# Three edits to a decoder trunk kernel: mask and maximum of a strip in one VectorE operation, the narrow column block of the projection first, the sample tile in halves

## The chip, the cores and the metric

The kernel runs on one core of one Trainium2 chip. The metric is the device time in microseconds; the median of the runs is compared. A core has TensorE (PE, matrix products into PSUM), VectorE (DVE), ScalarE (ACT) and GpSimd (POOL), a sync engine (SP) that issues most DMAs, a memory of 128 partitions (SBUF) and eight banks of 512 fp32 columns per partition into which products go (PSUM). All data is fp32.

## The reference, cut to what matters

One layer of a hybrid decoder trunk, for 1024 prompt tokens and 64 sample tokens (8 sequences of 8). Two pieces of it bear on the change. The first is the norm and the one combined input projection, of which the first 1304 columns (queries, keys and values of three branches, gates) are the attention part:

```python
n = rms_norm(x, lp['norm1_g'])
z = n @ lp['w_in']
z_attn, z_gate, z_rwkv = _split(z, [D_ATTN + 6 * D_KV, N_BRANCH * N_HEADS_ATTN, SHIFT_COLS])
```

The second is the sliding-window ("local") branch of prompt attention: a block of 128 queries against the 512 keys before it and its own 128, masked at both ends:

```python
s_w = jnp.einsum('bqghd,bkgd->bghqk', qg, win_kv[:, :, 0].astype(f32))
dist = q_pos[:, None] - w_pos[None, :]
p_w = masked_softmax(s_w, (dist >= 0) & (dist < WINDOW) & (w_pos[None, :] >= 0))
o_w = jnp.einsum('bghqk,bkgd->bqghd', p_w, win_kv[:, :, 1].astype(f32))
```

The rest (RWKV-7 time mixing of eight heads, compressed and selected branches, sample attention over a paged cache, output projection, an MLP of 4096) is computed by parts of the kernel that the change leaves alone.

## The kernel before, in words

Every engine has a program of its own, written out by hand in one order, with semaphores between them. The stages follow each other on TensorE: input projection, attention columns (to about 183 us), projection of the RWKV columns (to about 400), RWKV recurrence, compression of cache pages, prompt attention (850 to 1150), sample attention, output projection, MLP (from 1400 on).

**Projection.** Tokens lie in TILES = 9 tiles: eight of 128 prompt tokens and tile PT = 8 with the 64 sample tokens. The attention columns are in three BLOCKS (L503): 0 to 511, 512 to 1023 and 1024 to 1303. Weights of block b go to buffer b % 2. SP (L570 to L603) issues x tile 0, the norm's gain g1, the weights of block 0, the other x tiles, the weights of block 1, small constants, two weight tiles of the next stage, then waits for the first block's products before it issues the weights of block 2. ScalarE norms a tile (norm_rows, L900: square with sum, Ln, Exp, scaled copy), TensorE transposes it (turn_x, L1301: eight 128x128 transposes into banks 0 and 1, where each half waits until VectorE has read that bank's former tile), VectorE multiplies by g1 and writes nt (L2023). att_group (L1320) then makes the product of one tile and one block: eight k-steps, nt as the stationary operand, into one of three banks in turn; ScalarE evicts it (att_out, L917), which reorders the query columns of block 0. In the pass over the first block, TensorE's order (L1369 to L1374) is: turn tile 0, turn tile 1, group 0, turn tile 2, group 1 and so on. The other two blocks follow without transposes. For a sample tile the product has 64 rows, so half of the array's output columns. VectorE's head_sums(t) (L2042) waits until the third block of tile t is evicted.

**Prompt attention.** For each of eight query tiles i there are two units: "s" (selected branch, all i + 1 key tiles) and "cw" (compressed, then window, at most 5 key tiles). A unit has score steps, one for each pair of heads (two strips, g = 0 and 1, of up to 1024 columns), and the value steps of the unit before are spread between them (the list `order`, L458). With more than four key tiles the two strips fill banks 0 to 3, so the next scores (L1686) wait until both exponentials of the step are done. One step: TensorE writes the scores (L1703); VectorE adds the mask to both strips' edges in one operation (L2337 for full window strips, tiles 4 to 7; L2340 for the others) and takes the negated maximum of each strip (L2343); ScalarE computes exp(score - max) with its sum (exp_strip, L1170, the instruction on L1182). ScalarE's own order puts the two copies of a value step's transposed weights (v_copy, L1161, instruction on L1168) ahead of the first exponential, and where two value steps lie between two score steps the second's copies ahead of the second exponential.

`mm` (L1298) is the helper that issues every product, so products of all stages show as L1299. An fp32 product shows as two MATMUL instructions.

Of the kernel before, what the change touches and what calls it, by code (L numbers as in the profile page):

```python
# [15 lines left out]
P = 128  # L16
# [29 lines left out]
def rows(t):  # L46
    return P if t < PT else NS


def decode_trunk(nc, x_prompt, x_sample, cache_cmp_kv, cache_slc_kv, cache_win_kv, state_wkv, state_shift,  # L50
# [5 lines left out]
    with ctx:  # L56
# [214 lines left out]
        assert at[0] <= W0  # L271
        at[0] = W1
        ptb = [work(512) for _ in range(4)]
        qt = [work(HG, P) for _ in range(2)]
# [227 lines left out]

        BLOCKS = [(0, 512), (512, 512), (1024, ZA - 1024)]  # L503
        SPANS = [(0, 512), (512, 512), (1024, NS)]
# [42 lines left out]
        def _(sp):  # L547
# [21 lines left out]

            load_x(0)  # L570
            with nc.allow_non_contiguous_dma("small vectors, channel on the partition"):
                sp.dma_start(g1, norm1_g[0].rearrange("(k p) -> p k", p=P)).then_inc(sem("g1_in"), 16)
            load_w(0)
            for t in range(1, TILES):
                load_x(t)
# [316 lines left out]
        def _(act):  # L892
# [24 lines left out]
            def att_out(i):  # L917
                b, m = ATT[i]
                act.wait_ge(sem("proj"), i + 1)
                c0, n = BLOCKS[b]  # L920
                out, src = za[0:rows(m), m, c0:c0 + n], banks[2 + i % 3][0:rows(m), 0:n]
                if b == 0:

                    out = out.rearrange("p (h g d) -> p g h d", g=KVH, d=HD)
                    src = src.rearrange("p (g h d) -> p g h d", g=KVH, d=HD)
                nc.scalar.activation(out, src, ACT.Copy).then_inc(sem("att_out"), 1)  # L926
# [243 lines left out]
            def exp_strip(u, s, g):  # L1170
                i, kind = UNITS_A[u]
                x = no_s[u, s]
                act.wait_ge(sem("pa_max"), exps[x] + g + 1)
                if s == "c":
                    nc.scalar.activation(pc_r[i % 2], pc_r[i % 2], ACT.Exp).then_inc(sem("pa_p"), 1)
                    return
                br, hh = s
                if u >= 2 and hh == 0 and g == 0:
                    act.wait_ge(sem("turn_in"), after_unit(u - 2))
                h, w = head_of(hh, g), P * len(key_tiles(i, br))  # L1180
                s0 = strip_at(x)[0][g]
                nc.scalar.activation((pb_w if br else pb_s)[:, h, 0:w], psum[:, s0:s0 + w], ACT.Exp, bias=pmax[:, br, h:h + 1],  # L1182
                                     accum_out=psum_[:, br, h:h + 1]).then_inc(sem("pa_p"), 1)

# [112 lines left out]
        def _(pe):  # L1297
# [22 lines left out]
            def att_group(i):  # L1320
# [5 lines left out]
                ring_free(i)  # L1326
                n = BLOCKS[b][1]
                for k in range(KT):
                    ins = mm(banks[2 + i % 3][0:rows(m), 0:n], nt[:, k, m * P:m * P + rows(m)],
                             wb[b % 2][:, k, 0:n], k == 0, k == KT - 1)  # L1330
# [39 lines left out]
            turn_x(0)  # L1370
            for t in range(TILES):
                if t + 1 < TILES:
                    turn_x(t + 1)
                att_group(t)  # L1374
# [623 lines left out]
        def _(dve):  # L1998
# [313 lines left out]
            nc.vector.engine_nop().then_inc(once("q_zero")[0], 1)  # L2312

            def strip_max(u, s):
                i, kind = UNITS_A[u]
# [19 lines left out]
                if br == 1 and i >= WINDOW // P:  # L2335
                    ends = shaped3(strips, step // WINDOW, WINDOW)[:, :, :, 0:P]
                    link(tt(ends, ends, spread(edge_causal, 1, 2), ALU.add))  # L2337
                else:
                    ends = strips[:, :, w - P:w]
                    link(tt(ends, ends, spread(causal_add, 1, 2), ALU.add))  # L2340
# [278 lines left out]
```

## Time and profile before

| | us |
|---|---|
| median of the runs | 2261.91 (2259.36 to 2263.99, 3 runs) |
| the profiled execution | 2249.74 |
| its span | 2248.0 |
| TensorE busy | 2115.9 (94%) |
| VectorE busy | 1128.7 (50%) |
| ScalarE busy | 628.5 (28%) |
| GpSimd busy | 150.7 (7%) |

Times inside the profile are counted from the span's start. Busy time of TensorE is modelled at the ends of its instructions. An entry such as "x8" gives the number of instructions; "idle before" is the time that the engine stood still ahead of them, with the releaser behind the arrow.

### The profile page before, as it was taken

To read this page: it belongs to the slowest core of one execution; us is meant where nothing else is said; L and a number is where in the kernel's file an instruction comes from. 1 tells how busy PE (TensorE), PEld (TensorE's weight loads), DVE (VectorE), ACT (ScalarE), POOL (GpSimd) and SP (SyncE) were. 2 spreads that over 40 slices of the span, in tenths; PEclk is the share of its full clock that TensorE was granted. 3 is DMA by queue.
4 is the path that set the end of the run, shared out by engine and by line. 5 is a ranking of instruction groups with operands and counts; after the bars stand their busy time and mean duration, and the time that the engine had idled before them with its cause. 6 is when DMAs were issued, how large, how long until landed. Compare 5 with 4: busy or idle time off the path is not lost.

```text
span 2248.0 us, 36929 instructions
## 1 busy us (share of the span) xinstructions
PE 2115.9 (94%) x15228; PEld 1199.6 (53%) x15228; DVE 1128.7 (50%) x2278; ACT 628.5 (28%) x1408; POOL 150.7 (7%) x248
## 2 busy tenths in 40 slices
PE   7999999899998887888887899999999999999999
PEld 4456566799996774444344444444444444444443
DVE  2026664367665446766545313463636354554635
ACT  4113553222322115666543311202020111111110
POOL 3000000122222001211110000000000000000000
PEclk9999999999998997999998999999999999999999
DMA  6000112100012531000035421011111111111101
GB/s 189 21 1 19 29 29 88 68 4 22 4 23 77 170 96 54 10 5 5 5 113 154 129 75 61 11 60 42 38 38 38 38 38 38 38 38 38 38 38 80
DMA packets 99957, 115.72 MB, mean 51 GB/s; under 512 B 32243, under 2 KB 72116, under 8 KB 99726
## 3 DMA queue, kind: packets, MB, share of 16 engines
q1 hardware_dynamic: 95310, 106.01, 15.0%
q10 hardware_dynamic: 4480, 7.34, 1.1%
q8 instruction: 121, 1.98, 0.4%
q14 instruction: 46, 0.38, 0.1%
HBM read 104.75 MB, written 12.64 MB: 52 GB/s over the span
## 4 chain that ended last, share of the span: by engine, by line
PE 83%; DVE 6%; ACT 5%; DMA 2%; issue 2%; SPq 2%; ACTq 1%; POOL 0%; POOLq 0%; DVEq 0%
PE psum L1299 77%; PE psum L1724 2%; ACT arena L1182 2%; ACT arena L1168 1%; DMA arena<-in_cache_cmp_kv_dram 1%; SPq L702 1%; DVE arena L2343 1%; PE psum L1781 1%; PE psum L1622 1%; DVE arena L2369 1%; ACTq L1135 1%; DVE arena L2196 1%; DMA arena<-in_x_prompt_dram 0%; PE psum L1540 0%; SPq L646 0%
## 5 line engine op out<-in xcount | busy, mean ns | idle before, releaser
L1299 PE MATMUL psum<-arena 64*64 64x64 f32 (+12 forms) x12272 | 1863.6, 349 | 76.8 <-ACT arena L1182 44.0
L1299 PEld LDWEIGHTS psum<-arena 64*64 64x64 f32 (+5 forms) x12272 | 969.9, 152 | 872.5 <-issue 677.6
L2523 DVE TENSOR_TENSOR arena<-arena,psum 128x512 f32<-128x512 f32 x48 | 33.0, 688 | 305.8 <-PE psum L1299 305.8
L1280 ACT ACTIVATE arena<-psum 128x512 f32<-128x512 f32 x48 | 28.5, 594 | 420.0 <-PE psum L1299 327.3
L1271 ACT ACTIVATE arena<-arena 128x512 f32<-128x512 f32 x64 | 40.2, 628 | 274.2 <-DVE arena L2533 168.0
L1168 ACT ACTIVATE arena<-psum 128x512 f32<-128x512 f32 (+1 forms) x148 | 80.8, 595 | 86.3 <-PE psum L1724 74.4
L856 POOL TENSOR_TENSOR arena<-arena,m_lev 128x256 f32<-128x256 f32 x82 | 65.3, 797 | 586.2 <-DVE arena L2177 388.8
L1182 ACT ACTIVATE arena<-psum,arena 128x640 f32<-128x640 f32 (+7 forms) x128 | 88.8, 700 | 11.4 <-DVE arena L2343 10.9
L2343 DVE TENSOR_REDUCE arena<-psum 128x1 f32<-128x640 f32 (+7 forms) x128 | 84.6, 703 | 2.2
L2196 DVE TENSOR_TENSOR arena<-arena,psum 128x512 f32<-128x512 f32 x65 | 44.6, 687 | 74.2 <-PE psum L1299 73.5
L1048 ACT ACTIVATE arena<-psum 128x256 f32<-128x256 f32 x82 | 31.5, 384 | 171.4 <-PE psum L1299 171.4
L1724 PEld LDWEIGHTS psum<-ident,arena 128*128 128x128 f32 x528 | 59.1, 145 | 35.0 <-ACT arena L1168 15.4
L1724 PE MATMUL psum<-ident,arena 128*128 128x128 f32 x528 | 75.6, 288 | 2.1 <-DVE arena L2369 1.1
L2506 DVE TENSOR_TENSOR arena<-psum,arena 128x1024 f32<-128x1024 f32 x8 | 9.8, 1225 | 97.8 <-PE psum L1299 97.8
L1622 PE MATMUL psum<-ident,arena 128*128 128x128 f32 x272 | 42.6, 283 | 13.1 <-DVE arena L2266 13.1
L926 ACT ACTIVATE arena<-psum 128x512 f32<-128x512 f32 (+3 forms) x27 | 14.4, 532 | 133.2 <-PE psum L1299 133.2
L886 POOL TENSOR_SCALAR arena<-arena 128x640 f32<-128x640 f32 (+4 forms) x64 | 46.7, 741 | 49.1 <-DVE arena L2366 48.9
L1299 PE MATMUL psum<-ident,arena 64*64 64x64 f32 (+1 forms) x920 | 47.5, 223 | 2.5 <-DVE arena L2177 0.8
L1781 PE MATMUL psum<-ident,arena 128*128 128x128 f32 (+1 forms) x248 | 41.8, 307 | 8.4 <-DMA arena<-in_cache_slc_kv_dram 4.2
L2266 DVE COPY arena<-arena 128x512 f32<-128x512 f32 x68 | 27.9, 457 | 40.8 <-DMA arena<-in_cache_cmp_kv_dram 40.3
L1781 PEld LDWEIGHTS psum<-ident,arena 128*128 128x128 f32 (+1 forms) x248 | 29.5, 152 | 30.6 <-ACT arena L1217 14.6
L1299 PEld LDWEIGHTS psum<-ident,arena 64*64 64x64 f32 (+1 forms) x920 | 42.7, 139 | 4.4 <-DVE arena L2303 1.0
(311 smaller groups left out, 1717.8 us busy)
## 6 DMA issues: line engine op xcount, KB each, us to landing
arena<-in_cache_slc_kv_dram SPq DMA_DIRECT2D x128, 128.0 KB, 2.3
arena<-in_w_up_dram SPq DMA_DIRECT2D x7, 2048.0 KB, 7.4
arena<-in_w_down_dram SPq DMA_DIRECT2D x7, 2048.0 KB, 7.8
arena<-in_cache_cmp_kv_dram SPq DMA_DIRECT2D x72, 128.0 KB, 3.3
arena<-in_x_prompt_dram SPq DMA_DIRECT2D x16, 512.0 KB, 9.5
arena<-in_cache_cmp_kv_dram ACTq DMA_DIRECT2D x56, 128.0 KB, 3.1
arena<-in_w_in_dram SPq DMA_DIRECT2D x13, 512.0 KB, 3.9
arena<-in_w_in_dram SPq DMA_DIRECT2D x2, 2048.0 KB, 14.1
```

Source lines behind the costliest of these rows:

```text
L856: nc.gpsimd.tensor_tensor(amt[:, n % 2], atrb_r[c % 3][:, :, 0, :], spread(m_lev[:, i, :], 1, HP), ALU.mult).then_inc(sem("rw_amt"), 1)
L886: ins = nc.gpsimd.tensor_scalar(pb_w[:, h, 0:w], pb_w[:, h, 0:w], psum_[:, 1, h:h + 1], gates[:, i, 3 * h + 2:3 * h + 3], ALU.mult, ALU.mult)
L1168: nc.scalar.activation(ptb[2 * (st % 2) + g][0:p0], banks[4 + (f + g) % 2][0:p0], ACT.Copy).then_inc(sem("turn_out"), 1)
L1182: nc.scalar.activation((pb_w if br else pb_s)[:, h, 0:w], psum[:, s0:s0 + w], ACT.Exp, bias=pmax[:, br, h:h + 1], accum_out=psum_[:, br, h ...
L1271: link(nc.scalar.activation(block, block, ACT.Relu))
L1299: return nc.tensor.matmul(out, lhsT, rhs, start=start, stop=stop)
L1622: ins = nc.tensor.transpose(banks[g % 4][:, cols], by_head[a][x][:, cols], ident)
L1724: ins = nc.tensor.transpose(b[:, hh * P:(hh + 1) * P], (pb_w if s[0] else pb_s)[:, h, c0:c0 + P], ident)
L1781: ins = nc.tensor.transpose(b[0:t.shape[1], x * P:(x + 1) * P], t, ident)
L2196: tt(flat, flat, banks[4], ALU.subtract).then_inc(sem("rw_t"), 1)
L2343: nc.vector.tensor_reduce(pmax[:, br, h:h + 1], psum[:, s0[g]:s0[g] + w], AX.X, ALU.max, negate=True).then_inc(sem("pa_max"), 1)
L2523: tt(u2, t_sb, bank_of(6), ALU.add).then_inc(sem("u_sum"), 1)
```

## The change

Projection: the narrow block (280 columns) is the first of the three, and the two wide ones follow; x tile 1 is issued ahead of g1 and the weights; TensorE multiplies tile 0 ahead of transposing tile 1; the sample tile's product is made in two halves of the block's columns, one into partitions 0 to 63 and one into 64 to 127 of a bank, alternating k by k, and evicted with two copies. Window strips of tiles 4 to 7: a mask row of 640 columns is built once; one VectorE operation per strip adds it, negates, writes the strip back and gives the minimum, which is the negated maximum; the exponential of those strips takes scale -1.

```diff
+        window_add = region(R0 + HEADS * SEQ + HEADS * (WINDOW + P), WINDOW + P)
...
-        BLOCKS = [(0, 512), (512, 512), (1024, ZA - 1024)]
+        BLOCKS = [(1024, ZA - 1024), (0, 512), (512, 512)]
...
             load_x(0)
+            load_x(1)
...
-            for t in range(1, TILES):
+            for t in range(2, TILES):
                 load_x(t)
...
+                if m == PT:
+                    for h, half in enumerate(HALVES):
+                        out, src = za[0:NS, m, c0 + h * n // 2:c0 + (h + 1) * n // 2], banks[2 + i % 3][half, 0:n // 2]
+                        if c0 == 0:
+                            out = za[0:NS, m, 0:n].rearrange("p (h g d) -> p g h d", g=KVH, d=HD)[:, h]
+                            src = src.rearrange("p (h d) -> p h d", d=HD)
+                        ins = nc.scalar.activation(out, src, ACT.Copy)
+                    ins.then_inc(sem("att_out"), 1)
+                    return
...
+                turned_sign = br == 1 and i >= WINDOW // P
                 nc.scalar.activation((pb_w if br else pb_s)[:, h, 0:w], psum[:, s0:s0 + w], ACT.Exp, bias=pmax[:, br, h:h + 1],
-                                     accum_out=psum_[:, br, h:h + 1]).then_inc(sem("pa_p"), 1)
+                                     scale=-1.0 if turned_sign else 1.0, accum_out=psum_[:, br, h:h + 1]).then_inc(sem("pa_p"), 1)
...
+                if m == PT:
+                    for k in range(KT):
+                        for h, half in enumerate(HALVES):
+                            ins = mm(banks[2 + i % 3][half, 0:n // 2], nt[:, k, SEQ:], wb[b % 2][:, k, h * n // 2:(h + 1) * n // 2],
+                                     k == 0, k == KT - 1)
+                    ins.then_inc(sem("proj"), 1)
+                    return
...
             turn_x(0)
-            for t in range(TILES):
+            att_group(0)
+            turn_x(1)
+            for t in range(1, TILES):
                 if t + 1 < TILES:
                     turn_x(t + 1)
                 att_group(t)
...
+            link(nc.vector.memset(window_add, 0.0))
+            link(nc.vector.tensor_copy(shaped(window_add, WINDOW // P + 1, P)[:, 0::WINDOW // P, :], edge_causal))
...
                 if br == 1 and i >= WINDOW // P:
-                    ends = shaped3(strips, step // WINDOW, WINDOW)[:, :, :, 0:P]
-                    link(tt(ends, ends, spread(edge_causal, 1, 2), ALU.add))
+                    for g in range(KVH):
+                        h, strip = head_of(hh, g), psum[:, s0[g]:s0[g] + w]
+                        nc.vector.tensor_tensor_reduce(strip, strip, window_add, -1.0, -NEG, ALU.add, ALU.min,
+                                                       pmax[:, br, h:h + 1]).then_inc(sem("pa_max"), 1)
+                    return
```

## Rows read from the trace of the kernel before

**Rows 1.** The page: shares of the chain that ended last, by engine.
```profile
PE 83%; DVE 6%; ACT 5%; DMA 2%; issue 2%; SPq 2%; ACTq 1%; POOL 0%; POOLq 0%; DVEq 0%
```

**Rows 2.** Busy time by stretch: start:end, length, engines, granted clock, DMA share, GB/s.
```profile
200.00:300.00 100.00, 98.91 (x444) 59.20 (x443) 71.99 (x188) 55.41 (x142) 0.00 (x0) 1.00 0.12 31
300.00:400.00 100.00, 100.00 (x456) 61.24 (x455) 44.99 (x105) 38.36 (x106) 0.00 (x0) 1.00 0.24 75
...
1000.00:1100.00 100.00, 82.06 (x472) 40.74 (x471) 61.29 (x114) 60.51 (x123) 15.88 (x18) 0.98 0.02 6
```

**Rows 3.** TensorE groups by form, 0 to 175 and all; then timeline pieces.
```profile
L1299 PE MATMUL psum<-arena 128*64 128x512 f32 x32 | 14.2, 595 | 0.0
...
L1299 PE MATMUL psum<-arena 128*128 128x280 f32 x128 | 30.5, 400 | 0.0
...
L1299 PE MATMUL psum<-arena 128*64 128x280 f32 x16 | 4.0, 402 | 0.0
...
1396.79 7.09 PE L1299 MATMUL psum<-arena 128*64 128x512 f32 x32
...
845.99 0.42 PEld L1299 LDWEIGHTS psum<-arena,ident 128*64 128x64 f32 x8 [0.33 <-issue]
846.00 0.66 PE L1299 MATMUL psum<-arena,ident 128*64 128x127 f32 x8
```

**Rows 4.** Chain of waits of the first 160 us: start, length, what.
```profile
2.35 10.03 DMA arena<-in_x_prompt_dram
...
15.34 1.97 PE psum L1309 x8
17.31 7.34 PE psum L1299 x16
24.65 0.87 PE psum L1309 x8
25.52 6.87 PE psum L1299 x16
```

**Rows 5.** Timeline of the start, VectorE: start, length, engine, line.
```profile
8.97 1.44 DVE L2023 TENSOR_TENSOR arena<-psum,g 128x512 f32<-128x512 f32 x2 [3.27 <-PE psum L1309]
```

**Rows 6.** Stretches of 4 us with GB/s last; then issue to landing of the narrow block.
```profile
0.00:4.00 4.00, 0.00 (x0) 0.00 (x0) 1.71 (x7) 1.28 (x1) 2.58 (x17) 1.00 0.49 127
4.00:8.00 4.00, 0.26 (x2) 0.29 (x3) 1.53 (x6) 2.79 (x5) 2.97 (x18) 1.00 1.01 326
8.00:12.00 4.00, 1.68 (x8) 1.28 (x6) 1.38 (x2) 0.00 (x0) 3.32 (x11) 1.00 1.05 409
...
arena<-in_w_in_dram SPq DMA_DIRECT2D x1, 1120.0 KB, 5.1
```

**Rows 7.** VectorE and ScalarE groups by form, 800 to 1160: busy, mean ns, idle before.
```profile
L2343 DVE TENSOR_REDUCE arena<-psum 128x1 f32<-128x640 f32 x40 | 31.1, 820 | 0.7
...
L2337 DVE TENSOR_TENSOR psum<-psum,edge_causal 128x512 f32<-128x512 f32 x16 | 11.2, 700 | 31.7 <-PE psum L1299 31.7
...
L1182 ACT ACTIVATE arena<-psum,arena 128x640 f32<-128x640 f32 x40 | 31.5, 792 | 0.0
```

**Rows 8.** Timeline of one window step of tile 5.
```profile
1017.85 0.70 DVE L2337 TENSOR_TENSOR psum<-psum,edge_causal 128x512 f32<-128x512 f32 x1 [0.79 <-PE psum L1299]
1018.43 1.09 ACT L1168 ACTIVATE arena<-psum 128x512 f32<-128x512 f32 x2 [2.03 <-PE psum L1724]
1018.59 1.56 DVE L2343 TENSOR_REDUCE arena<-psum 128x1 f32<-128x640 f32 x2
...
1019.45 0.79 ACT L1182 ACTIVATE arena<-psum,arena 128x640 f32<-128x640 f32 x1
...
1020.23 0.78 ACT L1182 ACTIVATE arena<-psum,arena 128x640 f32<-128x640 f32 x1
...
1021.16 1.35 PE L1299 MATMUL psum<-arena 64*128 64x512 f32 x8 [1.32 <-ACT arena L1182]
```

**Rows 9.** Timeline around the gate into prompt attention.
```profile
852.64 0.43 DVE L2340 TENSOR_TENSOR psum<-psum,edge_causal 128x256 f32<-128x256 f32 x1 [3.53 <-PE psum L1299]
```

More of the change, by code:

```diff
@@ L272, in decode_trunk @@
         at[0] = W1
+        window_add = region(R0 + HEADS * SEQ + HEADS * (WINDOW + P), WINDOW + P)
+        assert R0 + HEADS * SEQ + (HEADS + 1) * (WINDOW + P) <= W0
         ptb = [work(512) for _ in range(4)]
@@ L920, in att_out @@
                 c0, n = BLOCKS[b]
+                if m == PT:
[7 more added lines that the diff above has]
+                    return
                 out, src = za[0:rows(m), m, c0:c0 + n], banks[2 + i % 3][0:rows(m), 0:n]
-                if b == 0:
+                if c0 == 0:
                     out = out.rearrange("p (h g d) -> p g h d", g=KVH, d=HD)
```

## The prediction

> **What bounds the kernel now.** The head of the page comes first: TensorE is busy 94% of a 2248.0 us span (the table above) and its instructions make up 83% of the chain that ended last; VectorE, which one edit touches, is busy 50% and holds 6% of that chain [rows 1]. The change lives in two places, so the table of stretches is read next, for those places only [rows 2]. In the projections TensorE has no room: 98.91 of 100 us in 200 to 300 and 100.00 in 300 to 400, with VectorE at 71.99 and 44.99. Work taken off TensorE here is therefore time gained, and so is an earlier start. In prompt attention (1000 to 1100) TensorE has 82.06 us of work, VectorE 61.29 and ScalarE 60.51: nobody is full, so a loop of latencies decides, and only the timeline of one step of that loop can tell what a faster VectorE is worth.
>
> The profiled execution took 2249.74 us (2248.0 of span and 1.7 around it), 0.5% under the median of the runs, 2261.91 (2259.36 to 2263.99). I work out differences in the profiled execution and take them off the median. A difference of 0.2% (4.5 us) is about the least that a measurement of this kernel can tell from none.
>
> **Part 1: the sample tile in halves.** Per column block, the sample tile is 8 k-steps whose weights are 128x64; each fp32 product shows as two matmul instructions, so 16 of them. In the first pass 32 such instructions of 512 columns cost 14.2 us, 0.444 each [rows 3], while the 16 of a full 128x128 product take 6.87, 0.43 each [rows 4]: half of the array's columns do nothing. In the narrow block 16 instructions of 280 columns cost 4.0 us. After the change there are 32 instructions per block at half the columns, and halves of the array alternate k by k. The row for that form is the sample tile of the output projection, which already does it: 32 instructions of 512 columns in 7.09 us, 0.222 each [rows 3]. At 256 columns that is 0.111 each, 32 x 0.111 = 3.55 us per wide block against about 6.95 (the average of 6.87 and 7.1); at 140 columns 32 x 0.061 = 1.95 against 4.0. Gain 3.4 + 3.4 + 2.05 = 8.8 us.
> What could spoil it is the doubled number of weight loads. Eight 128x64 loads took 0.42 us, 0.053 each, beside eight products in 0.66 us, 0.083 each [rows 3]. The wide blocks have 0.111 for each load, far enough; the narrow one has 0.061. Bounds: if 0.083 is the floor for the narrow block it takes 2.65 us and the gain is 8.1; if the halves did not overlap at all, each instruction of 256 columns costs half of 0.444 and the gain is zero. I take 8.8, by the row of the same alternation.
> The Trainium skill, "TensorEngine Tiling (Array Packing)", sections Key Properties and Restrictions, speaks against this edit: a change of tiling mode drains TensorE, and column tiling switches the fast weight load off. The sample tile before is 128x64 as well, so by that rule nothing is added but the loads, and the rows put these at 0.053 us; the sum stays as it is.
> Eviction: two ScalarE copies of half the columns instead of one, and ScalarE waits for TensorE there. Nothing.
>
> **Part 2: narrow block first, second x tile ahead of the weights, first product before the second transposes.** Rows 4 and 5 carry this. Before, the chain is: x tile 1 queues behind 2 MB of weights and lands at 12.37, its norm takes until 15.3, transposes 1.97, first product at 17.31 [rows 4]. Tile 0 had been normed and transposed by then and was written by VectorE at 8.97 + 1.44 = 10.41 [rows 5]; then TensorE waited 5 us for tile 1.
> After: tile 1 (0.52 MB) is second in the queue, the weights third and only 1.15 MB. By 4 us the queue had moved 127 x 4 = 0.51 MB, by 8 us another 326 x 4 = 1.30 MB, then 409 GB/s [rows 6]. Tile 1 is complete at 1.05 MB, about 5.7 us; the weights at 2.2 MB, 8 + 0.39/0.409 = 9.0 us. The same block alone took 5.1 us from issue to landing in the trace [rows 6], so short rows are no great handicap; bounds 8.8 to 10.5 (the 5.1 counted from 5.4, when tile 1 is nearly in). The small vector g1 now follows tile 1, about 6.5 us, and is wanted at 8.97. So the first group starts when VectorE has written tile 0, at 10.5.
> It is narrow: 16 x 0.238 = 3.8 us when TensorE is at speed [rows 3]. It won't be: transposes that take 0.87 in the stream took 1.97 at 15.34, and the first group 7.34 against 6.87 [rows 4], 1.57 us lost; the granted clock of this stretch reads 1.00 all the same, so I go by durations. I charge 1.2 us (bounds 0.5 to 1.9): the group ends at 15.5. ScalarE has normed tile 1 from 7.6 to 10.5 and tile 2 by 14. Transposes of tile 1 until 16.4; those of tile 2 share two banks with them, so their halves wait for VectorE's two writes of 0.69 us (16.0 to 17.4): they end at 17.9, with 0.7 us of stall. At 17.9 three tiles are turned and one narrow group is done. Before, at 17.31, two tiles were turned and no group done, and 0.47 us of cold were still to come. Gain: 0.87 + 3.8 + 0.47 - 0.59 = 4.6 us. Bounds 3 (weights at 10.5 and the cold charge at its top) to 5.5.
> Does the faster first pass starve? Its period falls from 6.87 + 0.87 = 7.74 to 3.8 + 0.87 = 4.67 us. ScalarE needs 0.40 to evict and 2.9 to norm a tile, 3.3; VectorE 1.3. x tiles arrive each 1.3 us. Slack 1.4 us. The second block's weights (2.1 MB) stand right behind the x tiles: 7.7 MB in all, 8 + 5.9/0.409 = 22.4 us by the rate of rows 6 (28 if it sags), and they are wanted at about 52. The third block, now 2 MB, is issued when the first pass is done (52) and wanted after the second (111); on SP's queue behind its wait stand only weight loads that wait for later products. The head sums of VectorE need all three blocks of a tile; the last block is now a wide one, so their tiles come every 6.87 us instead of every 3.8 and crowd it less than before (71.99 us busy in 200 to 300, with TensorE nearly full) [rows 2]. Nothing is next in line: the projection ends at about 169.5 instead of 183, and the rest moves up.
>
> **Part 3: mask and maximum in one VectorE operation.** 16 steps (tiles 4 to 7, four each). Removed per step: a mask add over 512 elements, 0.700 us, and two reductions over 640, 0.78 each (0.820 as the table's mean, which counts overlap) [rows 7]; 2.3 us. Added: two operations that read a PSUM strip and an SBUF row, write 640 elements to PSUM and give a minimum. The trace has none. From below: an add of 512 is 0.700 and a reduction of 640 is 0.820 [rows 7]; in pure proportion an add of 640 is 0.875, with a fixed part less, say 0.83; an accumulator read, if it comes as an instruction of its own as on ScalarE, overlaps or adds up to 0.2. From above: a second cycle per element gives 1.5. I take 0.95, nearest to the add.
> What is it worth? One step of the loop [rows 8]: the scores end at 17.8 (1017.8), VectorE adds until 18.55, its first maximum is ready at 19.4, its second at 20.15. ScalarE meanwhile copies two transposed banks, 18.43 to 19.52, starts the first exponential at 19.45, the second at 20.23, and TensorE's next scores wait for that one, 21.16. So the first maximum is hidden by the copies and the second by the first exponential. The table agrees: ScalarE idled 0.0 us before its 40 exponentials of 640 [rows 7]. A step that saves VectorE 0.4 us moves nothing. Value: 0, from -0.1 to +0.1 us per step. The cover is gone when two of the new operations last longer than 20.23 - 17.85 = 2.38 us, 1.19 each; in the 6 steps that have two value steps between their exponentials (1, 2 and 3 in tiles 5, 6 and 7) only past 1.75 each.
> The negated exponential costs the same. The two new operations before the first strip (a memset of 640, a copy of 256; under 1.3 us by the rows of adds) lie in the 3.53 us for which VectorE stood idle before 852.64, its first work in this stage [rows 9]; the gate that TensorE waits for is signalled ahead of them, and between it and 852.64 TensorE transposes, ScalarE copies and TensorE makes scores, some 1.9 us. Nothing.
>
> **Sum.** -8.8 - 4.6 - 0 = -13.4 us: 2261.9 - 13.4 = **2248.5 us**, 0.59% faster (the profiled execution would be 2236.3).
>
> **Rivals.** (a) *Two cycles per element for the fused operation*: 1.5 + 0.1 = 1.6 each, 3.2 per step against 2.38. Ten steps lose 0.8, six lose nothing: +8.2, so 2256.7. For it: it is a two-input operation with an accumulator and the trace shows no such thing; against: one input is in PSUM, and the two-input add of the trace, which reads PSUM and SBUF and writes PSUM too, takes 0.700 us for 512 elements [rows 7]. The Trainium skill, "Vector Engine (DVE) Microarchitecture Reference", section Points that are easy to get wrong, says that an accumulating two-source operation halves its rate when both sources are non-bf16 and in SBUF; here only one is, so by its letter the rule spares this operation, by its reason perhaps not. Chance 0.15.
> (b) *Slower than before: the fused operation takes over the loop.* At T us each the loss is 10(2T - 2.38) + 6(2T - 3.5) = 32T - 44.8; it eats 13.4 us at T = 1.82. At three cycles per element (2.15 us) it is +24, so 2272.5. Nothing in the trace points there; only that its price is unseen. Chance 0.06.
> (c) *The maximum does gate the loop*: then each of 16 steps gains the 0.6 us by which the first maximum is earlier, -9.6, so 2239. The 0.05 us between 19.40 and 19.45 is for it, the 0.0 idle against. Chance 0.06.
> (d) *The halves do not overlap*: -4.6 only, 2257. The row of 7.09 us is against it. Chance 0.05.
>
> **Chances and range.** Forecast 0.68, its own range 2244 to 2254 (the bounds of parts 1 and 2, 1.6 us of part 3 and 2 us of run-to-run median). For 8 in 10 it reaches down toward (c) and up over (a) and (d): 2242 to 2258. Faster by over 0.2% (below 2257.4): forecast, (c), three quarters of (a), half of (d), 0.87; within 0.2%: 0.07; slower: 0.06.
>
> **What would show it.** The products start at 10.5 and not 17.3; the sample group takes 3.5 us in wide blocks; projection ends near 169.5; TensorE stays at 100% to 400 us. In attention, scores still start every 4.71 us in the one-value steps, and ScalarE idles 0.0 before its 640-wide exponentials; VectorE's own busy time falls. If the period grows, the new operation is over 1.19 us; if it shrinks, I read the ScalarE cover wrongly. If weights land after 10.5 or TensorE stays slow longer, part 2 is smaller.

## The result and the profile after

The changed kernel took 2241.78 us (median of 7 runs, 2234.79 to 2247.9) beside 2259.61 for the kernel before (7 runs, 2255.53 to 2265.8): ratio 0.9922, 95% interval 0.9901 to 0.9943, so the medians lie 17.8 us or 0.8% apart. The forecast was 2248.5 with a range of 2242 to 2258: the direction was right, the range was missed by 0.2 us at its low end. More runs, told below, put the effect at 15 us and not 17.8.

The profiled execution took 2245.14 us, with a span of 2243.3. Where before and after can be compared mark by mark, its first 400 us are these:

| | before | predicted | after |
|---|---|---|---|
| first product starts | 17.31 | 10.5 | 10.45 |
| first group of the narrow block ends | | 15.5 | 16.01 |
| second group may start (three tiles turned) | | 17.9 | 18.49 |
| projection of the attention columns evicted | 183.2 | 169.5 | 171.0 |
| end of the projections | 406.6 | | 394.0 |

The chain of the page, the answer to [rows 1], says little: TensorE keeps its 83%, VectorE gives up a point.

```profile
PE 83%; DVE 5%; ACT 5%; issue 2%; DMA 2%; SPq 2%; ACTq 1%; POOL 0%; POOLq 0%; DVEq 0%
```

The chain of waits at the start answers [rows 4] (start, length, what):

```profile
0.82 3.70 DMA arena<-in_x_prompt_dram
...
7.64 1.95 PE psum L1322 x8
9.59 0.02 issue
9.62 0.70 DVE arena L2045
10.32 0.14 issue
10.45 5.56 PE psum L1312 x16
16.01 0.45 PE psum L1322 x4
16.46 0.02 issue
16.49 0.70 DVE arena L2045
17.19 0.14 issue
17.33 1.16 PE psum L1322 x8
18.49 3.78 PE psum L1312 x16
22.26 0.87 PE psum L1322 x8
```

The DMA of x tile 1 has left the chain. What follows tile 0 is VectorE's write of it, then the first group, which takes 5.56 us where the same group in the stream takes 3.78: 1.8 us lost to a TensorE that is not yet at speed, called the cold start below. TensorE's groups by form, 0 to 175 us, answer [rows 3]:

```profile
L1312 PE MATMUL psum<-arena 128*64 128x256 f32 x64 | 7.3, 382 | 0.0
...
L1312 PE MATMUL psum<-arena 128*64 128x140 f32 x32 | 2.1, 286 | 0.0
```

Two wide blocks of the sample tile take 7.3 us together, 3.65 each, and the narrow one 2.1; before, 14.2 and 4.0. The stretches answer [rows 2]; the second one stops being full only because the projections now end at 394:

```profile
200.00:300.00 100.00, 98.90 (x451) 58.52 (x450) 64.92 (x168) 52.68 (x135) 0.00 (x0) 1.00 0.12 32
300.00:400.00 100.00, 96.93 (x494) 60.27 (x494) 44.58 (x107) 34.90 (x102) 0.00 (x0) 1.00 0.27 91
1000.00:1100.00 100.00, 81.95 (x453) 40.06 (x452) 54.98 (x118) 59.73 (x120) 15.95 (x18) 0.97 0.02 6
```

In attention, VectorE fell from 61.29 to 54.98 us in 100, TensorE stands as it was. The groups by form of 800 to 1160 answer [rows 7] (busy, mean ns, idle before):

```profile
L1195 ACT ACTIVATE arena<-psum,arena 128x640 f32<-128x640 f32 x40 | 31.6, 800 | 0.0
...
L2363 DVE CUSTOM_DVE_ANT_0 psum<-psum,arena 128x640 f32<-128x640 f32 x32 | 25.8, 849 | 39.3 <-PE psum L1312 39.3
```

and the timeline of a step in tile 5 answers [rows 8]:

```profile
1003.01 0.83 DVE L2363 CUSTOM_DVE_ANT_0 psum<-psum,arena 128x640 f32<-128x640 f32 x1 [1.13 <-PE psum L1312]
1003.59 1.09 ACT L1180 ACTIVATE arena<-psum 128x512 f32<-128x512 f32 x2 [0.75 <-PE psum L1746]
1003.76 0.14 DVE L2363 DVE_READ_ACCUMULATOR2_ANT arena<- 128x1 f32 x1
1003.76 0.87 DVE L2363 CUSTOM_DVE_ANT_0 psum<-psum,arena 128x640 f32<-128x640 f32 x1
1004.54 0.14 DVE L2363 DVE_READ_ACCUMULATOR2_ANT arena<- 128x1 f32 x1
...
1004.56 0.80 ACT L1195 ACTIVATE arena<-psum,arena 128x640 f32<-128x640 f32 x1
...
1005.33 0.81 ACT L1195 ACTIVATE arena<-psum,arena 128x640 f32<-128x640 f32 x1
...
1006.28 1.35 PE L1312 MATMUL psum<-arena 64*128 64x512 f32 x8 [1.28 <-ACT arena L1195]
```

The first maximum is there at 1003.9, but ScalarE is busy with its copies until 1004.68 (1003.59 + 1.09, of which the last 0.12 overlap with what follows), so the first exponential starts at 1004.56, and TensorE waits for the second. Score steps with one value step between them start every 4.66 us instead of every 4.71.

The three edits met their marks, and the accounting closes up to 183 us: 13.4 predicted, less 0.6 of start, less 0.35 of the halves (3.65 and 2.1 for 3.55 and 1.95, three blocks), is 12.4; 183.2 - 171.0 = 12.2 is what the trace shows. But the profiled execution as a whole is only 4.6 us shorter than the profiled one before. The rest is lost here (start:end, length, five engines, granted clock): first before, then after, each in the same three stages, recurrence with cache pages, prompt attention, sample attention.

```profile
406.00:850.00 444.00, 410.76 (x8571) 371.98 (x8571) 259.37 (x546) 112.37 (x298) 76.04 (x95) 0.97 0.19 53
850.00:1149.00 299.00, 249.02 (x1435) 127.91 (x1434) 191.00 (x448) 182.54 (x428) 54.94 (x72) 0.94 0.05 15
1149.00:1305.00 156.00, 128.98 (x1330) 66.20 (x1329) 66.91 (x134) 49.74 (x92) 0.00 (x0) 0.89 0.47 143
```

```profile
394.00:838.00 444.00, 411.58 (x8568) 373.07 (x8569) 258.63 (x544) 112.62 (x298) 76.10 (x95) 0.97 0.19 53
838.00:1141.00 303.00, 252.90 (x1437) 129.46 (x1436) 181.73 (x466) 182.16 (x429) 55.20 (x72) 0.93 0.05 15
1141.00:1300.00 159.00, 130.30 (x1327) 66.64 (x1328) 66.56 (x134) 49.45 (x92) 0.00 (x0) 0.87 0.47 140
```

Two stages with idle time on TensorE took 303 and 159 us in place of 299 and 156, at granted clocks of 0.93 and 0.87 in place of 0.94 and 0.89. In prompt attention the place can be seen: the same step of scores, behind the same idle time of 1.76 us, first before, then after (start, length, idle before), with the stretch around it (granted clock behind the bracketed counts):

```profile
1037.35 1.78 PE L1299 MATMUL psum<-arena 64*128 64x512 f32 x8 [1.76 <-ACT arena L1182]
1033.00:1040.00 7.00, 5.24 (x32) 2.59 (x28) 3.31 (x5) 3.37 (x7) 0.76 (x1) 1.00 0.00 1
```

```profile
1027.10 3.15 PE L1312 MATMUL psum<-arena 64*128 64x512 f32 x8 [1.76 <-ACT arena L1195]
1025.00:1032.00 7.00, 5.24 (x22) 2.31 (x20) 2.58 (x4) 2.91 (x6) 0.00 (x0) 0.76 0.00 0
```

The step at 1040.85 took 3.25 us in the same way. This isn't of the change's making: another execution of the changed kernel (a2_whole below) took 1.78 us for both steps, and another one of the kernel before (b0_same) took 2.84 and 2.93. So the second question beside "do the mechanisms hold" is what the clock does to one run and to a median of a few.

### The profile page after: what moved, and what is told of

It is laid out like the page before. It is cut to its first block, busy times and chain, and to the rows that moved or that the text cites. A ratio compares the mean times of both kernels' runs of the same rounds, so it can differ in the third digit from the quotient of the medians.

```text
span 2243.3 us, 37047 instructions
## 1 busy us (share of the span) xinstructions
PE 2114.1 (94%) x15276; PEld 1201.3 (54%) x15276; DVE 1118.8 (50%) x2296; ACT 628.8 (28%) x1411; POOL 151.3 (7%) x248
## 3 DMA queue, kind: packets, MB, share of 16 engines
q10 hardware_dynamic: 4480, 7.34, 1.1%
## 4 chain that ended last, share of the span: by engine, by line
PE 83%; DVE 5%; ACT 5%; issue 2%; DMA 2%; SPq 2%; ACTq 1%; POOL 0%; POOLq 0%; DVEq 0%
PE psum L1312 77%; PE psum L1746 2%; ACT arena L1195 2%; ACT arena L1180 2%; SPq L705 1%; DMA arena<-in_cache_cmp_kv_dram 1%; PE psum L1803 1%; PE psum L1644 1%; DVE arena L2371 1%; ACTq L1147 1%; DVE arena L2397 1%; DVE arena L2218 1%; PE psum L1562 0%; PE psum L1322 0%; SPq L649 0%
## 5 line engine op out<-in xcount | busy, mean ns | idle before, releaser
L1312 PE MATMUL psum<-arena 64*64 64x64 f32 (+10 forms) x12320 | 1860.6, 349 | 77.2 <-ACT arena L1195 44.0
L1746 PEld LDWEIGHTS psum<-ident,arena 128*128 128x128 f32 x528 | 59.2, 146 | 35.5 <-ACT arena L1180 15.4
L2371 DVE TENSOR_REDUCE arena<-psum 128x1 f32<-128x128 f32 (+7 forms) x96 | 59.7, 663 | 1.7
L1644 PEld LDWEIGHTS psum<-ident,arena 128*128 128x128 f32 x272 | 34.1, 148 | 21.5 <-DVE arena L2288 14.4
```

The costliest lines, as they stand in the source:

```text
L1312: return nc.tensor.matmul(out, lhsT, rhs, start=start, stop=stop)
L1644: ins = nc.tensor.transpose(banks[g % 4][:, cols], by_head[a][x][:, cols], ident)
L1746: ins = nc.tensor.transpose(b[:, hh * P:(hh + 1) * P], (pb_w if s[0] else pb_s)[:, h, c0:c0 + P], ident)
L2371: nc.vector.tensor_reduce(pmax[:, br, h:h + 1], psum[:, s0[g]:s0[g] + w], AX.X, ALU.max, negate=True).then_inc(sem("pa_max"), 1)
```

## Experiments

"At the same clock" means below: a straight line fitted through all runs with a recorded clock, 197 of all kernels here (time against the run's mean granted clock, one level for each kernel), taken at clock 0.976. Its slope is -1.6 us for 0.001 of clock, and single runs scatter by 1.95 us (one standard deviation) around it. Clocks are recorded to 0.001.

**The parts.** e1_halves puts only the halved sample tile into the kernel before:

```diff
+                if m == PT:
+                    for k in range(KT):
+                        for h, half in enumerate(HALVES):
+                            ins = mm(banks[2 + i % 3][half, 0:n // 2], nt[:, k, SEQ:], wb[b % 2][:, k, h * n // 2:(h + 1) * n // 2],
...
```

> The kernel before with the sample tile in halves alone. My theory: two wide blocks save 3.4 us each and the narrow one 2.05, 8.8 us, ratio 0.9961; the profile's projection ends 8.8 us earlier and nothing else moves. Rival (weight loads limit the halves): under 5 us. Rival (the halves do not overlap): ratio 1.000.

Ratio 0.9964 (0.9949 to 0.9978), 12 runs; at the same clock 8.9 us under before (95%: 1.2 either way). In the profiled execution the attention columns were evicted at 176.4 in place of 183.2, although x tile 1 landed 0.4 us later and the first group took 8.57 us in place of 7.34: 6.8 + 0.4 + 1.2 = 8.4, by the trace alone. The halves overlap. The stretch from there to the end of the projections is 223.4 us here, in the kernel before, in e2_order and in the changed kernel alike, so the work behind the attention columns kept its length and only starts earlier.

e2_order has only the order of blocks, of x tile 1 and of the first group:

```diff
-        BLOCKS = [(0, 512), (512, 512), (1024, ZA - 1024)]
+        BLOCKS = [(1024, ZA - 1024), (0, 512), (512, 512)]
...
             load_x(0)
+            load_x(1)
...
+            att_group(0)
+            turn_x(1)
+            for t in range(1, TILES):
```

> The kernel before with the order alone: narrow block first, x tile 1 ahead of the weights, first product before the second transposes. My theory, with the cold charge that the changed kernel's profile shows (first group 5.56 us): 3.8 to 4.0 us, ratio 0.9983. Rival (the order is worth more than the start shows, since the head sums of VectorE get more room): over 6 us, and the stretch after the attention columns shorter too.

Ratio 0.9976 (0.9966 to 0.9986), 12 runs; at the same clock 5.7 us (1.2 either way) under before, more than the 3.8 to 4.0 expected. The rival that came with the expectation, more room for VectorE's head sums, is out by the 223.4 us just told. The profiled execution has its columns evicted at 180.7, only 2.5 us earlier, and its chain shows why: the same first group that took 5.56 above took 7.01 here.

```profile
10.46 7.01 PE psum L1300 x16
17.47 0.45 PE psum L1310 x4
```

Over several profiled executions, the projections end 12.6 us earlier with halves and order (four executions that start as before, seven that start as after), of which 8.4 are the halves: about 4.2 us for the order. The 1.5 us by which the times show more are not explained.

e3_fused has only the fused operation, its mask row and the scale of -1 in the exponential:

```diff
+                    for g in range(KVH):
+                        h, strip = head_of(hh, g), psum[:, s0[g]:s0[g] + w]
+                        nc.vector.tensor_tensor_reduce(strip, strip, window_add, -1.0, -NEG, ALU.add, ALU.min,
+                                                       pmax[:, br, h:h + 1]).then_inc(sem("pa_max"), 1)
+                    return
```

> The kernel before with mask and maximum in one operation alone. My theory: the loop is held by ScalarE's copies, so 0.05 us per step at most, 0.8 us in all, ratio 0.9996. Rival (the missing part of the measured 17.8 us is here): 4 to 5 us, ratio 0.998. Rival (two cycles per element): slower by 8.

Ratio 0.9992 (0.998 to 1.0005), 12 runs; at the same clock 0.2 us under before (1.2 either way), one-value steps at 4.66 us. Worth nothing that can be measured, as forecast. a2_whole is the changed kernel again:

> The changed kernel once more, beside its parts. If parts add up and the first 17.8 us held luck: 12.6 + 0.8 = 13.4 us, ratio 0.9941, and a profile in which the projection ends 12.6 us earlier as before while the later stages scatter by some us with the granted clock. If the change is worth more than its visible parts: ratio 0.992 or less again.

Ratio 0.9919 (0.9894 to 0.9944), columns evicted at 171.3. The three parts add at the same clock to 8.9 + 5.7 + 0.2 = 14.8; all 19 runs of the changed kernel, a3_whole below included, give 14.5 (1.0 either way). Nothing clear of the error is lost or won by having them together. The 0.9919 of a2_whole alone passed the mark that the expectation set for more than the visible parts (0.992 or less); a3_whole, at 0.9933, didn't, and the means of all runs (2242.0 beside 2257.0) give 0.9934.

**Is the fused operation really hidden?** e4_fused_longer lengthens VectorE's part: before each fused operation stands a reduction over the same strip whose result nobody reads.

```diff
+                        link(nc.vector.tensor_reduce(gtmp[:, 0, h:h + 1], strip, AX.X, ALU.max))
                         nc.vector.tensor_tensor_reduce(strip,
```

> The changed kernel with one more reduction over the 640 columns of a strip ahead of each fused operation (0.78 us; its result goes unused), so that a strip costs VectorE 1.6 us in place of 0.8. My theory of the cover (2.38 us for both strips of a step; 3.5 where two value steps lie in between): 10 steps lose 0.8 us, 6 lose nothing, 8 us slower than the changed kernel, and ScalarE idle before its 640-wide exponentials becomes 8 us. Rival (VectorE is never what the loop waits for): no difference. Rival (the maximum gates the loop already): 16 x 1.6 = 25 us slower.

Ratio to before 1.0015 (0.9999 to 1.003): 17 us slower than the changed kernel in the mean of the runs, 11 at the same clock. With 3.35 us of VectorE per step the cover of 2.38 us is gone and one-value steps take 5.72 us instead of 4.66, while two-value steps stay near 5.92. The expectation had 0.8 us for such a step, from 1.6 us per strip without the accumulator reads; 3.35 - 2.38 = 0.97 is nearer to the 1.06 measured. So the loop does turn on VectorE when it is made late enough. Ten steps of 1.06 us are 10.6, which is the difference at the same clock; the remaining 6 go with a lower clock (0.9729 against 0.9767 in the mean), and the trace shows places where it is lost: steps whose scores run slower. TensorE, 1014 to 1032 us (start, length, idle before):

```profile
1018.33 1.83 PE L1312 MATMUL psum<-arena 64*128 64x512 f32 x8 [2.35 <-ACT arena L1195]
1020.10 1.97 PE L1746 MATMUL psum<-ident,arena 128*128 128x128 f32 x8
1021.99 1.29 PE L1312 MATMUL psum<-arena 128*64 128x512 f32 x4
1024.53 1.35 PE L1312 MATMUL psum<-arena 64*128 64x512 f32 x8 [1.25 <-ACT arena L1195]
1025.81 1.09 PE L1746 MATMUL psum<-ident,arena 128*128 128x128 f32 x8
```

```profile
1018.00:1024.00 6.00, 4.96 (x20) 2.71 (x20) 4.26 (x11) 2.66 (x7) 1.28 (x2) 0.72 0.02 4
```

Eight transposes take 1.97 us and, a step later, 1.09; the granted clock of these 6 us averages 0.72, a mixture of its two levels of 1.2 and 2.4 GHz, and before them TensorE had stood idle for 2.35 us. All four window steps that stand behind 2.34 or 2.35 us of idle in this execution have such a stretch, at 0.72. But idle time alone doesn't decide it: behind 1.76 us the same step ran at either level in two executions of one kernel, as told above. That the longer idle lowered the clock of e4_fused_longer is therefore plausible and not shown.

**What holds the first exponential?** The prediction said: ScalarE's copies, which stand ahead of it. e5_exps_first puts both exponentials of a window step ahead of the copies in the changed kernel, e6_before_exps_first does the same in the kernel before:

```diff
+            if e[2] != "c" and e[2][0] == 1 and UNITS_A[e[1]][0] >= WINDOW // P:
+                act_order += [(x + 0.1, ("E", e[1], e[2], 0)), (x + 0.2, ("E", e[1], e[2], 1))]
+                continue
```

> The changed kernel with ScalarE's order altered for window strips of tiles 4 to 7: both exponentials of a step ahead of the copies of the value steps. My theory (the copies hold the first exponential for 0.7 us after the fused operation is done): the period of a one-value step falls from 4.66 to about 4.0, 6 to 10 us faster than the changed kernel, ratio to before about 0.990. Rival (the copies are then what TensorE waits for, at its next transposes): no gain or a loss of some us.

> The kernel before with the same altered order of ScalarE. My theory: its first maximum is ready only 0.05 us before the copies are done, so the new order has nothing to use: within 1 us of the kernel before, ratio 1.000. Rival (the order is worth the same without the fused operation): 6 to 10 us faster.

One-value steps fell from 4.66 to 4.05 us in e5 and stayed at 4.71 in e6: with the separate add and maxima VectorE is as late as the copies are, with the fused operation it is not. So the 0.6 us of the fused operation is real and lies behind ScalarE's order. The times did not follow: e5 0.9945 (0.9924 to 0.9966), no faster than the changed kernel, as its rival had it, and e6 1.0059 (1.0039 to 1.008), 12 us slower than before (10.0 at the same clock) where within 1 us was expected. The timeline of e5 shows what I had not counted, on TensorE ahead of a query turn and in a step with two value steps:

```profile
1012.21 0.66 PE L1702 MATMUL psum<-ident,arena 128*128 128x128 f32 x4 [1.15 <-ACT arena L1183]
...
1017.33 1.14 PE L1749 MATMUL psum<-ident,arena 128*128 128x128 f32 x8 [1.15 <-ACT arena L1183]
```

The next transposes want the bank that the delayed copies (L1183) read, and TensorE stands 1.15 us for them. In e6 the same transposes wait 1.81 us each, and no shorter step stands against it: from the first window step of tile 5 to the fourth score step behind it (1016.45 to 1037.35 in the kernel before) the kernel before takes 20.90 us and e6 23.33; the changed kernel takes 20.82 and e5 21.36. Three more kernels take this up, with one more copy of the changed kernel beside them. e8_mixed keeps the old order in the steps ahead of a query turn, and puts only the first exponential forward where two value steps follow; e10_single moves nothing but the seven one-value steps that stand ahead of no query turn:

```diff
+            if e[2] != "c" and e[2][0] == 1 and UNITS_A[e[1]][0] >= WINDOW // P and e[2][1] != 2 and len(vs) == 1:
+                act_order += [(x + 0.1, ("E", e[1], e[2], 0)), (x + 0.2, ("E", e[1], e[2], 1))]
+                continue
```

> The changed kernel; ScalarE's order is altered only in the window-strip steps of tiles 4 to 7 that do not stand before a query turn (12 of 16): the first exponential goes ahead of the value copies, the second ahead of them too where the step has one value step (7 steps), and behind the first pair of copies where it has two (5 steps). Theory (late copies hold TensorE only before a query turn and in steps of two values): the 7 steps take about 4.05 instead of 4.66 us, the others stay: 4.3 us less than the changed kernel, a ratio to the kernel before of about 0.9915, and no wait of 1.1 us on the copies. Rival (any reordering lets the clock drop and loses it again): no less than the changed kernel, about 0.993 to 0.994.

> Only the 7 one-value window-strip steps of e8_mixed have both exponentials ahead of the copies; the 5 steps with two values keep their order. Theory: the same 4.3 us as e8_mixed, since in a two-value step the copies and not the exponentials come last: ratio about 0.9915. Rival: the two-value steps profit from the earlier first exponential too; then e8_mixed is 1 to 2 us faster than this one.

> The changed kernel once more, beside the three others on the same chip. The theory of effect and clock (15 us less than the mean of the kernel before at the same mean granted clock) gives a ratio of 0.9933; the prediction's sum of 13.4 us gives 0.994; a value below 0.991 would say that more than the parts' sum is gained.

e10_single: 0.9925 (0.991 to 0.994). e8_mixed: 0.9943 (0.9918 to 0.9967). a3_whole: 0.9933 (0.9917 to 0.9949). At the same clock they are 18.7, 16.9 and 13.7 us under before (1.6 either way). The two reordered kernels were expected at 0.9915 and miss it; a3_whole is where it was expected. The step of e10 on ScalarE and TensorE:

```profile
1002.48 0.79 ACT L1198 ACTIVATE arena<-psum,arena 128x640 f32<-128x640 f32 x1 [1.40 <-DVE arena L2366]
...
1003.27 0.79 ACT L1198 ACTIVATE arena<-psum,arena 128x640 f32<-128x640 f32 x1
...
1004.05 1.08 ACT L1183 ACTIVATE arena<-psum 128x512 f32<-128x512 f32 x2
1004.20 0.30 PEld L1315 LDWEIGHTS psum<-arena 64*128 64x128 f32 x4 [1.54 <-ACT arena L1198]
1004.20 1.35 PE L1315 MATMUL psum<-arena 64*128 64x512 f32 x8 [0.66 <-ACT arena L1198]
```

ScalarE now waits 1.40 us for VectorE, the copies come last, and the period is 4.05 us; seven steps of 0.6 are 4.2 us, which is what e10_single shows over the changed kernel at the same clock (18.7 less 14.5, some 2 either way). In e8_mixed pairs of steps with two values in one of them are under 0.1 us shorter than in e10_single (11.40 and 11.49 us), so moving the first exponential there brought next to nothing. The four steps in tile 5 that took 20.82 us in the changed kernel take 20.20 in e10_single.

**The cold start.** e7_warm adds 25 transposes of the identity into a bank that nobody reads then: 20 before TensorE's first real transposes, 5 between these and the first group.

```diff
+            for _ in range(20):
+                nc.tensor.transpose(banks[7][:, 0:P], ident, ident)
             turn_x(0)
+            for _ in range(5):
+                nc.tensor.transpose(banks[7][:, 0:P], ident, ident)
```

> The changed kernel with 20 transposes of the identity ahead of the first tile's, and 5 more between these and the first product (their result goes unused), so that TensorE is at work from 2.3 us on. My theory (half clock is what makes the first group 5.56 us and the first transposes 1.94): first group 3.8, first transposes near 1.0, 1.8 to 2.7 us faster than the changed kernel. Rival (the first group waits for its weights as they land): still over 5 us, no gain.

Its TensorE at the start (start, length, idle before):

```profile
2.46 4.53 PE L1391 MATMUL psum<-ident 128*128 128x128 f32 x20 [2.46 <-POOL num L805]
7.81 1.09 PE L1322 MATMUL psum<-ident,arena 128*128 128x128 f32 x8 [0.82 <-ACT arena L910]
8.74 0.71 PE L1394 MATMUL psum<-ident 128*128 128x128 f32 x5
10.18 4.04 PE L1312 MATMUL psum<-arena 128*128 128x280 f32 x16 [0.73 <-DMA arena<-in_w_in_dram]
```

The first group takes 4.04 instead of 5.56 us, the first transposes 1.09 instead of 1.95, and the columns are evicted at 169.2 instead of 171.0, 0.3 us before the prediction's 169.5. The ratio is 0.9931 (0.9914 to 0.9948). The trace shows 1.8 us; the times can hardly resolve that, but agree: at the same clock 16.7 us under before, 2.1 more than the changed kernel, some 1.8 either way.

**Together, and the kernel before against itself.** e9_mixed_warm is e8_mixed with the 25 transposes, e11_single_warm is e10_single with them, b0_same is the kernel before, unchanged.

> The edit of e8_mixed together with the 25 unused transposes of e7_warm. Theory: the two gains lie in different stages and add: 4.3 and 1.8 us less than the changed kernel, a ratio of about 0.9905. Rival: as for e8_mixed, then only the 1.8 us of the start, about 0.9925.

> The edit of e10_single together with the 25 unused transposes of e7_warm. Theory: the gains of the two stages add: at the same mean granted clock 18.4 us (e10_single) and 1.8 us (the start) under the kernel before, about 2236.5 us beside 2256.7, a ratio of 0.991. Rival (the clock takes back what idle time is removed elsewhere): as the changed kernel, about 0.9935.

> The kernel before against itself, nothing changed. The theory of the miss (a median of a few runs strays by several us with the mean granted clock, so that 2261.91 lay about 5 us too high as a base): single runs between 2249 and 2266 us, falling 1.6 us per 0.001 of clock, medians of 5 runs up to 3 us apart, ratio between 0.9985 and 1.0015. Rival (2261.91 was the kernel's time on its chip, and the chips differ): all runs of this chip within 2 us of one value, whatever their clock.

e9_mixed_warm: 0.9915 (0.9891 to 0.9939). e11_single_warm: 0.9935 (0.991 to 0.9959); at the same clock 22.1 and 18.6 us (1.8 and 1.7 either way). Expected were 0.9905 and 0.991; the parts would add to some 18.7 and 20.5, so the two scatter about it on either side. In plain time none of the four kernels e8 to e11 is clearly faster than the changed one: their 24 runs average 2241.8 us, the 19 of the changed kernel 2242.0, and their clock 0.9740 against 0.9767. By the slope that lower clock is worth 4.3 us, as much as the loop gained at the same clock. That the shorter steps lowered the clock is not shown: no stretch of the traces was found where it falls in each run.

b0_same against the kernel before: 1.0001 (0.999 to 1.0013). Its twelve runs, by clock:

```
clock 0.973 to 0.975   2263.07  2259.31  2261.12
clock 0.976 to 0.977   2257.14  2255.44  2254.93  2259.20  2255.54
clock 0.979            2254.36  2257.90  2256.12  2256.07
```

One kernel on one chip strays over a range of 8.7 us, and most of it goes with the clock. All 88 runs of the kernel before that have a recorded clock lie between 2249.74 (the profiled execution of the forecast, at 0.979) and 2264.02, with a mean of 2257.0; time and clock correlate at -0.85, 1.5 us for 0.001. The rival in its recorded form (all runs of a chip within 2 us of one value) falls; a small difference between chips doesn't: at the same clock the means of four chips are 2256.7, 2257.2, 2257.7 and 2258.2. The seven runs of the kernel before in the first comparison have no recorded clock and are not among the 88. They average 2260.4 (2255.53 to 2265.8), and with them the mean is 2257.2; that a low clock made them so slow is likely by the rest, but not shown.

## Why the prediction was right and where it was wrong

**What bounds the kernel: right.** Work taken off TensorE in the projections came back one for one, and VectorE's saving in attention was covered.

**Part 1, the halves: right.** Predicted 8.8, measured 8.9 in the times and 8.4 in the trace. (The working's average of 6.87 and 7.1 is 6.99, not 6.95, which moves the gain by under 0.1.) The output projection's sample tile was the right row to scale from; 3.65 and 2.1 us against 3.55 and 1.95. The doubled loads cost 0.15 us in the narrow block. The Trainium skill, "TensorEngine Tiling (Array Packing)", section Key Properties, has a change of tiling mode drain TensorE; the trace bears out that nothing is added for it here, since beyond the 0.15 us nothing is seen. Rival (d) is out.

**Part 2, the order: right in place, short in one term.** The first product started at 10.45 against 10.5, and behind VectorE's write as the prediction has it. The weights were nearly last themselves: in the chain of e7_warm they land at 10.14 (2.20 + 7.94), not at 9.0, inside the bounds and hidden by 0.3 us. Under-sized was the charge for a TensorE that isn't at speed: 1.2 us (bounds 0.5 to 1.9) against 1.8 in the profiled execution, and in eight profiled executions with this order and no added transposes (of six kernels) the first group took 5.51, 5.56, 5.87, 6.16, 6.22, 6.58, 7.01 and 7.06 us, 1.7 to 3.3 over the 3.78 of the stream. I had read the charge from one execution of before, in which the first group was the shortest that I have seen: 7.34, against 7.55, 7.99, 8.13 and 8.57 in four other executions that start as it does. Both sides stood too low, so the difference suffered less: 4.2 us by the ends of the projections in several traces, and 5.7 (1.2 either way) in the times, against 4.6.

**Part 3, the fused operation: right.** I took 0.95 us between 0.83 and 1.5; it takes 0.83 to 0.87, with an accumulator read of 0.14 that overlaps the next operation. That is the rate of the masked add before (0.700 us for 512 elements), so rivals (a) and (b) are out, and the halved rate that the Trainium skill's "Vector Engine (DVE) Microarchitecture Reference", section Points that are easy to get wrong, gives for two non-bf16 sources in SBUF does not show with one of them in PSUM. Rival (c) is out too, and e5 against e6 shows why: the copies hold the first exponential. One thing was too flat: "0, from -0.1 to +0.1" named no price for the cover. It is 0.6 us per one-value step, to be had only with ScalarE's order changed as well.

**The sum: right within its error.** 13.4 predicted; 15.0 in the mean of all runs, 14.5 (1.0 either way) at the same clock. The 1.1 to 1.6 us between are not in the projections, which gave less than 13.4 (12.6 us between 406.6 and 394.0, 12.9 between the means of four executions of before's start and three of the changed kernel); 0.4 or so is the 0.05 us of the one-value steps. The rest, 1 to 2 us, is not settled; the error of the times is 1.0.

**The step that failed: the base.** "I work out differences in the profiled execution and take them off the median", with "2 us of run-to-run median" in the range. The median of three runs was 2261.91; 88 runs average 2257.0 (95 with the first seven, 2257.2). From that base the same sum gives 2243.6, beside 2242.0 measured over 19 runs. The forecast was 6.7 us too high, and 4.9 of them are the base; the other 1.8 lie in the sum, within its error. The sign stood in the text itself: the profiled execution, 2249.74, lay 12 us under the median, and I gave it a sentence and no weight. A spread of 14 us between four executions (2249.74 to 2263.99) calls, by my estimate from these four, for some 4 us on each side for the base alone, twice what I allowed, and for a centre between 2249.74 and 2261.91. The 17.8 us of the first comparison is the same effect: its seven runs of the kernel before have a median of 2259.61, 2.6 us over the mean of the 88, while its median after, 2241.78, is within 0.2 us of the 2242.0 of all. That the base was too high is measured; why it was is open, since those runs have no recorded clock.

## What to carry to other kernels

Before a difference is taken off a median, look how far the profiled execution lies from it and at the granted clock of both: here 0.001 of clock went with 1.6 us, and the spread of the base was larger than the error of the sum. When an operation is shortened in a loop of latencies, follow the next engine's order of work to what really releases it, and price the cover: the shorter operation is worth something only together with a change of that order, and every instruction that the change delays has readers of its own. Charge a start-up cost from more than one execution.

## What the runs showed of the hardware that was not expected

- Two sources, one in PSUM and one in SBUF, with an accumulated minimum and the destination in PSUM: 0.83 to 0.87 us for 640 fp32 columns, no more than the add alone by proportion; the accumulator read is a separate instruction of 0.14 us, and the next operation starts beside it.
- TensorE is slow at its first real work although the granted clock reads 1.00 for the stretch: 5.51 to 7.06 us for a group that takes 3.78 later, and 4.04 with 25 small transposes before it. The variation between executions, 1.55 us, is nearly as large as the cost, 1.7 to 3.3.
- The same score step behind the same 1.76 us of idle on TensorE took 1.78 us in some executions (before, e3_fused, a2_whole, e10_single) and 2.84 to 3.25 in others (after, a3_whole, b0_same, e8_mixed), at a granted clock, over the 7 us around it, of 1.00 (before) and 0.76 (after, a3_whole, b0_same). Executions of one kernel differ in this.
- The lowest mean clocks were those of two kernels with a changed attention loop: 0.9729 for e4_fused_longer and e8_mixed, against 0.9764 before. In e4 that is plausible from the longer idle; in e8 the loop had less idle, e5_exps_first, which moves more, stands at 0.9757, and the cause is open.
